# Projection and decode attention in one stage of a hybrid decoder step on one Trainium2 core

## The reference

```
h = rms_norm(x, norm_mix)                        # 288 x 1024
proj = h @ w_in                                  # 1024 -> 3600: conv q,k,v (1536), z (512), ba (16), q,k,v (1536)
conv_out = silu(causal_conv4(proj_conv, state))  # 12 tiles of 128 channels
qg, kg = l2_normalize(conv_out q, k)             # per head of 64; then the gated delta rule
beta = sigmoid(b);  g = -exp(a_log) * softplus(a + dt_bias)
gate = silu(z)                                   # used on the normed output of the delta rule
# decode attention, per sequence: 1024 cached positions (8 pages of 128 x 512) and 4 new tokens
z[t,s] = q_t . k_s / 8 + b_h                     # past keys and new keys
A[t,s] = sigmoid(z[t,s]) * prod_{s<j<t} (1 - sigmoid(z[t,j]))
o_t = sum_s A[t,s] v_s
x = x + concat(o_gdn, o_attention) @ w_out
x = x + moe(rms_norm(x))                         # 32 experts, 4 per token
```

## Time and profile before

| | |
|---|---|
| median of three runs | 1309.69 us (1308.79 to 1310.25) |
| profiled execution, span | 1313.2 us |
| TensorE busy | 1253.0 us (95%) |
| VectorE busy | 402.9 us (31%) |
| ScalarE busy | 247.9 us (19%) |
| GpSimd busy | 97.3 us (7%) |
| DMA | 463.64 MB, mean 353 GB/s |

### The profile page before, as it was taken

One profiled execution on the slowest core, in us unless ns is written; L12 is line 12 of the kernel. 1 busy time (PEld: TensorE's weight loads), 2 busy tenths in 40 slices (PEclk: granted clock), 3 DMA queues, 4 the chain that ended last, 5 costly groups with the idle time before them and its releaser, 6 DMA issues.

```text
span 1313.2 us, 20103 instructions
## 1 busy us (share of the span) xinstructions
PE 1253.0 (95%) x7924; PEld 566.2 (43%) x7924; DVE 402.9 (31%) x912; ACT 247.9 (19%) x416; POOL 97.3 (7%) x172
## 2 busy tenths in 40 slices
PE   8999998989999999999999999999999999999996
PEld 6777775687443333333333333333333333333332
DVE  4721343642742222322222232222213322212323
ACT  3223332623211110110111011011101101011103
POOL 6101142252000000000000000000000000000000
PEclk9999998999989999999999999999999999999999
DMA  9643699020799999999999999999999999999994
GB/s 319 237 128 92 226 373 339 9 88 7 280 334 382 425 428 429 426 429 428 428 430 425 429 428 424 431 428 429 425 430 429 426 430 426 430 427 427 429 427 185
DMA packets 68156, 463.64 MB, mean 353 GB/s; under 512 B 16910, under 2 KB 17038, under 8 KB 41478
## 3 DMA queue, kind: packets, MB, share of 16 engines
q1 hardware_dynamic: 64536, 451.17, 83.9%
q0 software_dynamic: 3520, 11.54, 2.4%
q10 hardware_dynamic: 46, 0.18, 0.0%
HBM read 459.15 MB, written 3.70 MB: 352 GB/s over the span
## 4 chain that ended last, share of the span: by engine, by line
PE 55%; DMA 23%; issue 1%; ACT 1%; DVE 0%; SPq 0%; DVEq 0%; ACTq 0%
PE bank L2130 25%; DMA ring<-in_w_up 20%; PE bank L2163 6%; PE bank L2099 4%; PE bank L2078 4%; PE bank L2143 3%; PE bank L1588 2%; DMA ring<-in_w_down 2%; PE bank L2082 1%; PE bank L2103 1%; PE bank L1453 1%; PE bank L1443 1%; PE bank L1450 1%; PE bank L2190 1%; PE bank L2119 0%
## 5 line engine op out<-in xcount | busy, mean ns | idle before, releaser
L2130 PE MATMUL bank<-ring,work 128*64 128x512 f32 x1280 | 288.5, 604 | 19.4 <-DMA ring<-in_w_up 19.4
L2130 PEld LDWEIGHTS bank<-ring,work 128*64 128x64 f32 x1280 | 91.7, 139 | 213.5 <-issue 202.9
L2163 PE MATMUL bank<-ring,work 128*64 128x512 f32 x768 | 172.3, 596 | 7.7 <-ACT work L2265 5.3
L410 PE MATMUL bank<-hoT,ring 128*128 128x288 f32 x448 | 115.1, 412 | 0.8 <-ACT hoT L445 0.5
L2163 PEld LDWEIGHTS bank<-ring,work 128*64 128x64 f32 x768 | 54.8, 137 | 103.4 <-issue 98.7
L410 PEld LDWEIGHTS bank<-hoT,ring 128*128 128x128 f32 x448 | 84.9, 193 | 23.7 <-issue 0.7
L2364 DVE TENSOR_SCALAR work<-bank 128x512 f32<-128x512 f32 x32 | 22.1, 690 | 231.5 <-PE bank L2143 230.5
L2249 ACT ACTIVATE work<-bank 128x1024 f32<-128x1024 f32 x16 | 16.4, 1024 | 385.9 <-PE bank L2082 365.1
L2323 DVE TENSOR_TENSOR X<-X,bank 128x512 f32<-128x512 f32 x64 | 44.0, 688 | 120.7 <-PE bank L2099 120.7
L2377 DVE COPY work<-bank 128x512 f32<-128x512 f32 x16 | 11.1, 692 | 211.5 <-PE bank L2163 211.5
L2099 PE MATMUL bank<-work 128*128 128x512 f32 x128 | 59.2, 605 | 0.0
(11 more groups left out here) (414 smaller groups left out, 1396.2 us busy)
## 6 DMA issues: line engine op xcount, KB each, us to landing
ring<-in_w_up SPq DMA_DIRECT2D x96, 2048.0 KB, 24.7
ring<-in_w_down SPq DMA_DIRECT2D x48, 2048.0 KB, 26.6
work<-in_w_up SPq DMA_DIRECT2D x16, 2048.0 KB, 24.2
hoT<-in_w_up SPq DMA_DIRECT2D x16, 2048.0 KB, 28.6
work<-in_w_down SPq DMA_DIRECT2D x16, 1024.0 KB, 22.7
hoT<-in_w_down SPq DMA_DIRECT2D x16, 1024.0 KB, 24.6
ring<-in_w_in SPq DMA_DIRECT2D x7, 2048.0 KB, 16.0
ring<-in_cache_k SPq DMA_DIRECT2D x48, 256.0 KB, 3.0
```

The costliest lines, as they stand in the source:

```text
L410: ins = pe.matmul(bank[0:m, i % 2, 0:T], w[:, k, :], hT[:, k, :], start=k == 0, stop=k == KD - 1)
L2130: ins = pe.matmul(bank[CAP * e:CAP * e + CAP, g, :], xT[:, k, CAP * e:CAP * e + CAP], weight(odd, ch + e, k % 2 * RSLOT + 512 * g), start= ...
L2163: ins = pe.matmul(bank[CAP * e:CAP * e + CAP, 4 + m, :], aT[:, k, CAP * e:CAP * e + CAP], weight(odd, ch + e, k % 4 * D + 512 * m), start= ...
```

## The change

Blocks 1 and 2 become one block.

- The order of tiles is now q, k, v, ba, conv 0 to 11, z. All loads of the block stand in one list, `PAIRS`, and go through six slot pairs in its order: pair q may be loaded when pair q - 6 is used up. SyncE loads the weight groups, the keys (each sequence of eight pages a pair) and `w_out`; the numbers of the pages are read first, all eight, then the wait, then the eight DMAs. The page table is asked for ahead of the first group.
- Keys: each page goes into 32 partitions x 4 x 512 (rows of the page four to a partition), and VectorE turns the whole pair in place in blocks of 32 x 32, two instructions of 2048 columns a sequence (`turn_keys`, L857). TensorE's transposes and the copies of ScalarE and VectorE are gone. The scores (L450) are sixteen matmuls of 256 columns a sequence, with the queries spread over `Q32`, which stands in `Xw` where x and the norm's row stood; GpSimd clears it, ScalarE writes it, and x is loaded a second time at the end (`load_x`).
- Sequences are handled in four pairs b: scores(b), weights(b), turn_A(b), values(b), own_heads(b), put between the projection tiles by number (`if i == ...`).
- GpSimd loads all value pages (`load_values`): sequences 0 to 2 ahead of the first silu product, 3 behind silu(1), 4 and 5 behind silu(4) and silu(5), 6 and 7 behind silu(7) and silu(8).
- The silu product moves from VectorE to GpSimd (three instructions a tile), the final scaling of q and k from GpSimd to VectorE (four of 576 columns). The conv is one chain of four instructions on 312 columns, prompt and decode together, and its state is turned in one transpose a tile.
- The gate of z moves into block 3: a sigmoid on ScalarE and a product that is VectorE's last there (L1286, L1375).

The core of the diff:

```diff
-        GROUP_COL = [0, GW, 2 * GW, C_Z, C_S, C_S + GW, C_S + 2 * GW]
...
-        CACHE_UNITS = [("k", 0, 1), ("k", 0, 0), ("v", 0, 1), ("k", 1, 1), ("v", 0, 0), ("k", 1, 0), ("v", 1, 1), ("v", 1, 0)]
...
+        PAIRS = [("w", "q"), ("K", 0), ("K", 1), ("w", "k"), ("K", 2), ("K", 3), ("w", "v"), ("V", 0), ("V", 1), ("K", 4), ("K", 5),
+                 ("w", "c0"), ("V", 2), ("V", 3), ("w", "c1"), ("K", 6), ("K", 7), ("w", "c2"), ("V", 4), ("V", 5), ("w", "z"),
+                 ("V", 6), ("V", 7), ("o", 0), ("o", 1)]
+        NPR = NSLOT // 2
...
+        def load_values(eng, n, used):
+            q = pair("V", n)
+            pages = [eng.value_load(pt[0:1, NPG * n + pg:NPG * n + pg + 1], min_val=0, max_val=POOL - 1) for pg in range(NPG)]
+            used(eng, q - NPR)
+            if n >= 2:
+                eng.wait_ge(v_sem(n), v_count(n - 2))
+            for pg, page in enumerate(pages):
+                eng.dma_start(pair_tile("V", n)[:, GW * pg:GW * (pg + 1)],
+                              cache_v[0, bass.ds(page, 1)].rearrange("o p h d -> (o p) (h d)")).then_inc(v_sem(n), 16)
...
-        tiles = [("conv", j) for j in range(12)] + [("ba", 0)] + [("z", j) for j in range(4)] + \
-                [("q", j) for j in range(4)] + [("k", j) for j in range(4)] + [("v", j) for j in range(4)]
+        tiles = [("q", j) for j in range(4)] + [("k", j) for j in range(4)] + [("v", j) for j in range(4)] + [("ba", 0)] + \
+                [("conv", j) for j in range(12)] + [("z", j) for j in range(4)]
...
+                        for pg, page in zip(KEY_PAGES, pages):
+                            kb, odd = pg // 2, pg % 2
+                            sp.dma_start(tile[32 * kb:32 * kb + 32, 4 * GW * odd:4 * GW * (odd + 1)].rearrange("p (q c) -> p q c", q=4),
+                                         cache_k[0, bass.ds(page, 1)].rearrange("o (q r) h d -> (o r) q (h d)", q=4)).then_inc(done, 16)
...
+                    if PAIRS[q] == ("K", 5):
+                        sp.wait_ge(s_tte, K_TURNED)
+                        store_kv(kst, k_prompt, k_sample, s_kout)
+                    if PAIRS[q] == ("V", 3):
+                        sp.wait_ge(s_tte, V_TURNED)
+                        store_kv(vs_tok, v_prompt, v_sample, s_vout)
+                    if PAIRS[q] == ("V", 7):
+                        sp.wait_ge(s_sc, NSEQ)
+                        load_x()
...
+                        keys = pair_tile("K", s).rearrange("p (g c) -> p g c", g=8)
+                        for m in range(4):
+                            for j in range(HP):
+                                cb = 4 * j + m
+                                ins = pe.matmul(bank[32 * j:32 * j + 32, 6, 256 * (s % 2):256 * (s % 2) + 256]
+                                                .rearrange("p (g r) -> p g r", g=8), Q32[:, s, cb, :], keys[:, :, 32 * cb:32 * cb + 32],
+                                                start=m == 0, stop=m == 3)
+                        ins.then_inc(s_sc, 1)
...
+                    for kb in range(4):
+                        for e in range(2):
+                            for c in range(2):
+                                s, pg = 2 * b + e, 2 * kb + c
+                                w = P * (2 * e + c) + 32 * kb
+                                ins = pe.matmul(bank[64 * e + 32 * c:64 * e + 32 * c + 32, 3, :], AT[:, w:w + 32], pair_tile("V", s)[:, GW * pg:GW * pg + GW],
+                                                start=c == 1 and kb == 0, stop=kb == 3)
...
+                    if i == 6:
+                        scores(0)
+                    if i == 8:
+                        new_scores()
+                    if i == 9:
+                        scores(1)
+                    if i == 10:
+                        spread_new()
+                    if i == 12:
+                        turn_A(0)
+                    if i == 14:
+                        values(0)
+                        scores(2)
+                    if i == 16:
+                        turn_A(1)
+                        own_heads(0)
+                    if i == 17:
+                        values(1)
+                    if i == 19:
+                        turn_A(2)
+                        own_heads(1)
+                        scores(3)
+                    if i == 20:
+                        values(2)
+                    if i == 22:
+                        turn_A(3)
+                        own_heads(2)
+                    if i == 24:
+                        values(3)
+                        square_sums(range(3))
+                    if i == 25:
+                        square_sums(range(3, 5))
+                    if i == 26:
+                        own_heads(3)
+                        square_sums(range(5, 8))
...
+                    if i == 25:
+                        conv_sigmoid(11)
+                        gate_inputs()
+                        for k in range(2):
+                            log_squares(k)
+                    if i == 26:
+                        for k in range(2, 6):
+                            log_squares(k)
+                    if i == 27:
+                        copy_heads_out(3)
+                        for k in range(6, 8):
+                            log_squares(k)
+                        act.wait_ge(s_rt, 8)
+                        for n in range(4):
+                            act.activation(l2[:, 2 * n:2 * n + 2, :], l2[:, 2 * n:2 * n + 2, :], ACT.Exp, scale=-0.5).then_inc(s_rt, 1)
...
+                def silu(j):
+                    pool.wait_ge(s_sg, j + 1)
+                    x, g = cbuf[j % 2], csig[j % 2]
+                    pool.tensor_tensor(gq[:, j, 0:SEQ], x[:, 0:SEQ], g[:, 0:SEQ], ALU.mult)
+                    (x0, x1), (g0, g1) = own_steps(x), own_steps(g)
+                    pool.tensor_tensor(gq[:, j, SEQ:T - NDEC].rearrange("p (s i) -> p s i", i=NDEC), x0[:, :, 0:NDEC], g0[:, :, 0:NDEC], ALU.mult)
+                    pool.tensor_tensor(gq[:, j, T - NDEC:T], x1, g1, ALU.mult).then_inc(s_silu, 1)
+                pool.wait_ge(s_pt, 16)
+                for n in range(3):
+                    load_values(pool, n, used)
+                for j in range(12):
+                    silu(j)
+                    if j == 1:
+                        load_values(pool, 3, used)
+                    if j in (4, 5):
+                        load_values(pool, j, used)
+                    if j in (7, 8):
+                        load_values(pool, j - 1, used)
+                    if j == 0:
+                        pool.wait_ge(s_kout, 32)
+                    if 0 < j <= 8:
+                        pool.wait_ge(s_silu, j)
+                        if j == 1:
+                            pool.wait_ge(s_tt, V_TURNED)
+                        pool.tensor_tensor(l2[:, j - 1, :], gq[:, j - 1, 0:T], gq[:, j - 1, 0:T], ALU.mult).then_inc(s_sq, 1)
...
+                def turn_keys(s):
+                    pair_wait(dve, "K", s)
+                    for h in range(2):
+                        v = pair_tile("K", s)[:, 2 * PAST * h:2 * PAST * (h + 1)]
+                        ins = dve.transpose(out=v, in_=v)
+                    ins.then_inc(s_kt, 1)
...
+                    for w in range(CONV):
+                        sc = convw[:, j, w:w + 1]
+                        if w == 0:
+                            c(dve.tensor_scalar(o, px[:, 0:CW], sc, None, ALU.mult))
+                        else:
+                            ins = dve.scalar_tensor_tensor(out=o, in0=px[:, w:w + CW], scalar=sc, in1=o, op0=ALU.mult, op1=ALU.add)
+                            if w < CONV - 1:
+                                c(ins)
+                            else:
+                                ins.then_inc(s_cv, 1)
...
+                    if i == 4:
+                        turn_keys(2)
+                    if i == 5:
+                        turn_keys(3)
+                    if i == 7:
+                        mask_new()
+                    if i == 8:
+                        weights_new()
+                    if i == 9:
+                        products_new()
+                        weights(0)
+                    if i == 10:
+                        turn_keys(4)
+                    if i == 12:
+                        abs_a()
+                        turn_keys(5)
+                    if i == 14:
+                        weights(1)
+                    if i == 15:
+                        own(0)
+                    if i == 17:
+                        weights(2)
+                    if i == 18:
+                        own(1)
+                        turn_keys(6)
+                    if i == 19:
+                        turn_keys(7)
+                    if i == 21:
+                        own(2)
+                        weights(3)
+                    if i == 25:
+                        own(3)
+                        log_gates()
...
+                act.activation(zs, zg, ACT.Sigmoid).then_inc(s_zs, 1)
...
```

(2 more changed lines are left out.)

886 lines of the change are left out of this document (393 added, 493 removed).

## The result

The changed kernel took 1354.0 us (median of four runs, 1352.2 to 1356.1) against 1310.0: a ratio of 1.033 with the interval 1.031 to 1.035. The forecast was 1315.4 with 1300 to 1333; it was right that the kernel would be slower, and wrong in by how much.

The account below looks back on a forecast made before the run. TensorE was taken to bound the two stages before the experts. Profiled span 1313.2 - 7.6 (merged stage) + 1.3 (gate) + 12 (clock) = 1318.9, or 1315.4 us on the runs' scale; eight in ten from 1300 to 1333.

Parts of the forecast that it names:

- the 15 charged for the clock inside it: Merged stage: work lost to a lower granted clock behind waits, 4 us at each of three places and 3 early.
- the profiled execution is 3.5 above the median: Last step of the sum: conversion from the profiled span, 1318.9 us, to the runs' scale, 1315.4.
- The small ones I estimate at 9.2.: TensorE's small work in the merged stage: turning weights, own-head products, square sums, conv state turns; 9.2 of 157.5 us.
- I take the full rate for the forecast: Key page loads into 32 partitions: assumed as fast as on 128, 5.4 us a sequence and not 9.6.
- Rival A: Key pages on 32 partitions load slowly, at 221 GB/s, delaying the weight groups: +13, 1328 us; chance 0.26.
- ends 31.2, lands 33.7: V3's pages, us from the first conv tile: last issue ends, data lands 2.5 later; TensorE waits 4.7 at values(1).
- V5 and V7, 4.4 and 8.2 forecast: TensorE's waits at values(2) and values(3) for pages GpSimd issues between silu products: 4.4 and 8.2 us.
- the logarithms: ScalarE's gate and L2 logarithms at tiles 25 to 27, with two table loads, make TensorE wait 4.8 us.
- Rival C: VectorE's key turns cost twice, 8.8 us a sequence, delaying scores(3) and the first pairs: 1325 us; chance 0.07.
- The clock, +12 forecast: Granted clock falls behind TensorE's waits: 15 us lost in the merged stage, 3 given back in the third; bounds 0 and 20.
- The relief in the third stage, -3: Start of the third stage: 3 us of clock loss given back because the idle stretch ahead is shorter.
- Rival B: The granted clock stays up, so the 12 us fall away: 1300.5 us; chance 0.28 with a milder form at 1306.

Follow-up runs that it names:

- early loads: Changed kernel with the k group first, V3 behind silu(0), key pages on 128 partitions and fixed page numbers: 1306.4 us, 0.9965 of the kernel before.

## Why the prediction was wrong

The merged stage was to end at 212.3, and at 227.3 with the 15 charged for the clock inside it. It ended at 263.7. By the terms of the sum:

| term | forecast | measured |
|---|---|---|
| start | 15.0 | 14.6 |
| TensorE's own work at full clock | 157.5 | 167.8 |
| clock loss in the stage | 15 | 22.4 |
| idle, with the stage's end | 39.8 | 58.9 |
| sum | 227.3 | 263.7 |

The measured total of the runs is 38.6 above the forecast: 36.4 by the merged stage, 4.1 less behind it, and 6.3 by the step "the profiled execution is 3.5 above the median", which took the distance between a span and a median from an execution of before that was 5 above its own; the median of the changed kernel is 2.8 above its span.

- **Own work, +10.3: mis-sized.** "The small ones I estimate at 9.2." With tiles, scores and values as forecast and 4.2 for the new tokens they come to 17.4: the turns of the new k and v rows (eight of 0.49) were not counted, a turn of weights took 1.06 and not 0.66, the own-head products 0.96 and not 0.6. The new tokens' products took 1.05 a pair at full clock, not 0.5 (4.2 for 2.1). A tile (4.0), scores (3.66 a pair) and values (3.64) came as in the earlier trace rows.
- **The waits for weights, 4 forecast and 23.8 measured** (10.9, 3.4, 9.6). The step that failed is "I take the full rate for the forecast". The state load of the earlier trace rows was the right bound: its 221 GB/s at a full share is near the 240 measured at a share of 1.07. I set its rate down to its small pieces as well as its partitions; the 64-partition run, with pieces of 2 KB and 242 GB/s at 1.07, shows that the partitions were enough. Rival A had the mechanism, and its 9, 6 and 5 for the three waits add up to 20 of the 23.8 measured; the price of the whole, 13, was not: the destination was worth 16 to 24. What the Trainium skill states in *SBUF — State Buffer*, as the prediction cites it, spoke for A, and I gave it a quarter.
- **The full rate was not the only thing wrong there.** With key pages on 128 partitions tile 4 still waited 8.0 us and tile 13 3.0. The k group was asked for at 30.4, as forecast, but took 10.6 us to land and not 7 (a sum with a start of 1.6 that no row shows): K1 was still landing, and K2 was asked for behind it.
- **V3, 4.7 forecast and 12.6 measured.** The step "ends 31.2, lands 33.7" took a landing on an idle queue. V3's pages were issued while K6 was still landing and page by page beside K7, 4 MB of keys that were needed 30 us later than V3, and TensorE waited until 11.6 after their last issue. The schedule had each queue's order, but not what the DMA still had to move. Asked for 8 us earlier, ahead of K7, V3 made the kernel 9.3 faster.
- **V5 and V7, 4.4 and 8.2 forecast, 1.6 and 4.6 measured.** The costs of GpSimd were right (8.4 a sequence for 9.2), but TensorE came later, by the clock and the turns.
- **Right as sized:** the turns (2.28 each, forecast 2.2) and the first wait for them (2.7 for 2.8), the second 2.9 for 4.8; the last weights 3.3 for 3.4; the logarithms 4.8 for 4.8; the end 2.5 for 2.7; the gate's product, VectorE's last step of the third stage, 1.40 for 1.3. Rival C is out, by the 2.28 of a turn.
- **The clock, +12 forecast.** The falls that were placed came (tile 4, V3, the turns and V5, V7, the logarithms), but that behind V3, put down as a small one, was among the longest, and those behind the waits for the v group and the first conv group were not placed. Counting them beside the waits was wrong in kind: as long as loads set the pace the stage ended no earlier when 8 of the 22 us were given back. And its price was read from one execution that was 5 us above the median. The relief in the third stage, -3, was -3.1 with the gate's 1.4 in it, and that was luck: with the same work ahead of it the third stage took 45.3 to 46.9 in seven of seventeen profiles, about what it took before (45.6).
- **Rival B** (the clock stays up) is out for the changed kernel; 1297, its figure, came only with early loads and TensorE kept at work, that is by another way.
- **The range.** Its upper end, 1333, was A with 5 more. A had the forecast's clock in it, so it was not the mixing of cases that failed but what both shared. From A's 1328 to 1354 it is 26: 10.3 of own work, 7.4 of clock, 6.1 of waits (A took the wait for V3 as 3 smaller, and it was 8 larger), 6.3 by the scale of the runs, less 4.1 behind the stage and 0.4 at its start. The range had room for the rival's price, and none for a sum of small works that was too low by half.

## What to carry to other kernels

When work leaves the bounding engine, list for each load not only when it can be asked for, but what the DMA has still to move at that moment, and whether what stands ahead is needed later than what stands behind: one place in GpSimd's order was worth 9 us, and taking work off VectorE cost 8 because a weight group for later got ahead of value pages. A layout that saves an engine its turns by loading into a part of the partitions pays for it in DMA time; price it from the nearest row with few partitions, not from full tiles. Where a profile is a single execution, first compare its time with the median, before taking a price from a stretch, or the distance from span to median, that may not be in every run.

## What the runs showed of the hardware that was not expected

- Pages of 256 KB in pieces of 2 KB, in part beside a weight group, moved at 348 GB/s on 128 partitions, 242 on 64, 240 on 32 with the halves in turn and 215 on 32 with neighbours in a row, from 48 to 56 us of four variants, at shares of 0.99 to 1.07. The pages of K2 landed 0.68, 1.09, 1.09 and 1.25 us apart. A busy share of 1 says nothing of the rate.
- A page number read by SyncE took some 0.6 us, by GpSimd 0.46 (3.7 for eight), about as long as the issue of the page itself (0.48 and 0.58).
- TensorE's granted clock was 0.50 to 0.58 behind waits of 9 to 13 us; with early loads and extra matmuls in the remaining waits it was 1.00 on the mean of the stage. That gave back ten us where little but TensorE set the pace, and eight us given back where loads did changed nothing.
- The same 12 us of work ahead (busy 4.0, 4.0 and 1.5 of three stretches of 4 us) were followed by a granted clock of 1.00 in ten profiles and of 0.50 to 0.67 in seven, which made the stage behind 2.8 to 4.4 us longer.
